# Gated delta rule: key-key and key-query products made once per token tile and kept in SBUF for the other scan direction

## The chip, the cores and the metric

One core of a Trainium2 chip runs the whole program. The metric is the device time of one execution in microseconds; the time of a kernel is the median of its runs.

## What is computed

The reference is a four-layer transformer for one latent sequence of 256 tokens and one context of 256 tokens, all in float32. Layer 1 is a gated delta network with 8 heads of dimension 128, and the change lies in it alone. It is scanned in both directions. For one head, one direction and one chunk, cut to what matters:

```python
decay = where(tri, exp(gc[:, None] - gc[None, :]), 0)     # gc: running sum of the gates, per direction
lmat  = where(strict, (k * beta) @ k.T * decay, 0)
tmat  = inverse(eye + lmat)
a_qk  = q @ k.T * decay
v_new = tmat @ (v * beta) - (tmat @ (k * beta * exp(gc))) @ state
o     = (q * exp(gc)) @ state + a_qk @ v_new
state = state * exp(gc[-1]) + (k * exp(gc[-1] - gc)).T @ v_new
```

`k @ k.T` and `q @ k.T` don't depend on the direction. `beta`, `gc`, the triangle and the state do.

## The kernel before

The kernel is written engine by engine: every engine has its own program, and counted semaphores order them. The 512 tokens are 4 tiles of 128. After the projections of layer 1 comes the scan: the loop over `s` (4 steps) and, inside it, over `hg` (two groups of 4 heads). One pass of the inner loop is called a half-step here; there are 8. A half-step treats both directions d = 0 and d = 1, each on its own tile: `tls = (s, s ^ 1)`, so direction 0 visits tiles 0, 1, 2, 3 and direction 1 visits tiles 1, 0, 3, 2. What direction 0 uses in an even step is thus used by direction 1 in the odd step after it, and the other way round.

PSUM has 8 banks of 128x512. Direction d uses bank 3d, 3d+1 and 3d+2, and bank 6+d. The four heads of a group lie side by side in a bank, 128 columns each. A half-step runs in this order:

- TensorE makes the decay rows (L1607, bank 3d; from the second half-step on each direction waits for its state update `st_upd` first), the key-key products (L1611, bank 3d+1), and behind both directions the key-query products (L1615, bank 3d+2).
- VectorE subtracts and clamps them (L2385, `bD`), ScalarE takes the exponentials (L945 to `bD`, L946 to `bE`), VectorE multiplies decay, -beta and key-key product to `bNL` (L2393, one instruction for each head, the product read from PSUM), then the masked decay with the key-query product to `bAT` (L2400, one 128x512 instruction for each direction).
- GpSimd has two instructions for each direction: it masks the decay (L699, `bAT` from `bD`, as soon as L945 is done) and multiplies `bE` with the queries (L706). All of them read SBUF.
- TensorE inverts by levels: L1636 (needs `bNL`) into bank 3d, which ScalarE copies (L952) to `bA`; key times state (L1624) into bank 6; L1647 and L1651, which need `bAT`'s bank read and `bA`, into banks 3d+1 and 3d+2; L1624 again for the other direction; VectorE copies (L2405, L2408) and adds values (L2417); L1660, L1665 and L1672; then L1680 solves, L1687 and L1688 give the outputs, L1694 the state product, L2435 or L2437 and L2443 store and update (no state update in step 3).

The order within each engine is that of its program text. The matmuls are float32; each one of the source stands as two records in the trace. `w_hi` and `w_lo`, which hold the split weights of the projections, are idle during the scan: GpSimd begins the next split when the last output of the scan is ready. No DMA is issued for the scan.

Of the kernel before, what the change touches and what calls it, by code (L numbers as in the profile page):

```python
# [19 lines left out]
ALU = mybir.AluOpType  # L20
ACT = mybir.ActivationFunctionType
# [5 lines left out]
P = 128  # L27
# [155 lines left out]
def build(nc, a, out):  # L183
    with ExitStack() as ctx:
        top = [nc.sbuf_base + (-nc.sbuf_base) % 64]

        def sb(name, shape, dt=F32, at=None):
            size = int(np.prod(shape[1:])) * (1 if dt == U8 else 4)
            if at is None:
                at = top[0]  # L190
                top[0] += (size + 63) // 64 * 64
            assert at + size <= nc.sbuf_usable_end, (name, at + size)
            return nc.alloc_sbuf_tensor_at(name, shape, dt, offset=at)

        sem = lambda n: ctx.enter_context(nc.semaphore(n))
        banks = ctx.enter_context(nc.psum_tensor("bank", [P, 8, 512], F32))
        bank = [banks[:, i, :] for i in range(8)]
# [11 lines left out]
        WH0 = top[0]  # L209
# [25 lines left out]
        K4 = 2048  # L235
# [37 lines left out]
        bt = [[sb(f"b{n}{d}", [P, 4, P], at=U0 + (3 + 6 * d + i) * K4) for i, n in enumerate(("D", "E", "AT", "NL", "TT", "A"))]  # L273
              for d in range(2)]
        bT = sb("bT", [P, 4, P], at=U0 + 15 * K4)
        Z0, E0 = AR0, AR0 + 32 * K4
        ZF = 32 * 33
        zg, zb = (sb(n, [P, 2, 32], at=B0 + 256 * i) for i, n in ((0, "zg"), (1, "zb")))
# [119 lines left out]
        qd_ready = sem("decayed_queries_ready")  # L398
        kk_ready = sem("key_products_ready")
        kq_ready = sem("query_products_ready")  # L400
        at_ready = sem("attention_ready")
        nl_ready = sem("lower_ready")
        a_ready = sem("level_a_ready")
# [71 lines left out]
        quad = lambda t: t.rearrange("p (a b) -> p a b", a=4)  # L475
# [302 lines left out]
        def _(eng):  # L778
# [86 lines left out]
            def delta_net():  # L865
# [55 lines left out]
                for s in range(TT):  # L921
                    for hg in range(2):
                        first = (s, hg) == (0, 0)
                        for d in range(2):
                            TTm = bt[d][4]
                            th = 8 * (s if d == 0 else s ^ 1) + 4 * hg
                            if first:
                                eng.wait_ge(zt_ready, act.next(zt_ready))
                            else:
                                eng.wait_ge(ty_ready, act.next(ty_ready))  # L930
                            for g in range(4):
                                R = slice(32 * g, 32 * g + 32)
                                turn = lambda t: t[R, :, th:th + 4].rearrange("p c t -> p t c")
                                ins = eng.activation(TTm[R, :, R], turn(bTT32[d]), ACT.Copy)
                                if g // 2 == d:
                                    ins = eng.activation(bT[R, :, R], turn(bT32[d]), ACT.Copy)
                            ins.then_inc(diag_ready, 1)
                        for d in range(2):
                            Dm, E = bt[d][0:2]
                            if (s, hg) == (TT - 1, 1):  # L940
                                eng.wait_ge(od_ready, 14)
                            elif not first:
                                eng.wait_ge(s_done, act.next(s_done))
                            eng.wait_ge(dm_ready, act.next(dm_ready))
                            eng.activation(Dm[:], Dm[:], ACT.Exp).then_inc(dt_ready, 1)  # L945
                            eng.activation(E[:].rearrange("p a b -> p (a b)"), bank[3 * d][:], ACT.Exp).then_inc(e_ready, 1)  # L946
                        for d in range(2):
                            Am = bt[d][5]
                            eng.wait_ge(a_ready, act.next(a_ready))
                            for q in range(2):  # L950
                                S, T = slice(64 * q + 32 * d, 64 * q + 32 * d + 32), slice(64 * q + 32 - 32 * d, 64 * q + 64 - 32 * d)
                                ins = eng.activation(Am[T, :, S], quad(bank[3 * d][T, :])[:, :, S], ACT.Copy)  # L952
                            ins.then_inc(am_ready, 1)
                        for d in range(2):
                            Am = bt[d][5]
                            S, T = slice(64 * d, 64 * d + 64), slice(64 - 64 * d, 128 - 64 * d)
                            eng.wait_ge(a_ready, act.next(a_ready))
                            eng.activation(Am[T, :, S], quad(bank[3 * d][T, :])[:, :, S], ACT.Copy).then_inc(am_ready, 1)
# [244 lines left out]
        def _(eng):  # L1203
# [339 lines left out]
            def delta_net(l):  # L1543
                inside = late_beside(l)
                for p in range(16):
# [10 lines left out]
                    if p == 1:  # L1556
                        ada_late(l, 13, 14, 15)
                        eng.wait_ge(tz_ready, pe.next(tz_ready))
                        for t in range(TT):
                            mm = eng.transpose(bank[6][:, t * B_TAIL:(t + 1) * B_TAIL], btz[:, t * P:(t + 1) * P], ident[0:B_TAIL, 0:B_TAIL])  # L1560
# [16 lines left out]
                    if p == 6:  # L1577
                        eng.wait_ge(hn_ready, pe.next(hn_ready, 2))
                        eng.wait_ge(sm_b, pe.next(sm_b, 2))
                        for th in range(32):  # L1580
                            tl, h = divmod(th, B_HEADS)
                            for g in range(4):
                                blk = bk[:, h, tl * P + 32 * g:tl * P + 32 * g + 32]
                                mm = eng.matmul(bank[4 + th // 16][32 * g:32 * g + 32, th % 16 * 32:th % 16 * 32 + 32], blk, blk, start=True, stop=True)
# [9 lines left out]
                for s in range(TT):  # L1594
                    for hg in range(2):
# [5 lines left out]
                        C = lambda b: slice(b * P, (b + 1) * P)  # L1601
                        for d in range(2):
                            if not first and (s, hg) != (TT - 1, 1):
                                eng.wait_ge(st_upd, pe.next(st_upd))
                            for b in range(4):
                                c = d * B_HEADS + H(b)
                                mm = eng.matmul(bank[3 * d][:, C(b)], b_g[:, tls[d], c:c + 1].to_broadcast([P, P]), con[:, tri[d]:tri[d] + P],  # L1607
                                                start=True, stop=True)
                            mm.then_inc(gb_ready, 1)
                            for b in range(4):  # L1610
                                mm = eng.matmul(bank[3 * d + 1][:, C(b)], bk[:, H(b), tok[d]], bk[:, H(b), tok[d]], start=True, stop=True)  # L1611
                            mm.then_inc(kk_ready, 1)
                        for d in range(2):
                            for b in range(4):
                                mm = eng.matmul(bank[3 * d + 2][:, C(b)], bk[:, H(b), tok[d]], bq[:, H(b), tok[d]], start=True, stop=True)  # L1615
                            mm.then_inc(kq_ready, 1)
# [23 lines left out]
                        for d in range(2):  # L1640
                            TTm, Am = bt[d][4:6]
                            eng.wait_ge(diag_ready, pe.next(diag_ready))
                            eng.wait_ge(at_ready, pe.next(at_ready))
                            eng.wait_ge(am_ready, pe.next(am_ready))
                            for b in range(4):
                                i, o = 96 * d, 32 + 32 * d
                                eng.matmul(bank[3 * d + 1][o:o + 32, b * P + i:b * P + i + 32], TTm[o:o + 32, b, o:o + 32],  # L1647
                                           Am[o:o + 32, b, i:i + 32], start=True, stop=True)
                                for q in range(2):
                                    i, o = 64 * q + 32 * d, 64 * q + 32 - 32 * d  # L1650
                                    mm = eng.matmul(bank[3 * d + 2][i:i + 32, b * P + o:b * P + o + 32], Am[o:o + 32, b, i:i + 32],  # L1651
                                                    TTm[o:o + 32, b, o:o + 32], start=True, stop=True)
                            mm.then_inc(b_ready, 1)
# [9 lines left out]
                        for d in range(2 if s < TT - 1 else 0):  # L1663
                            for b in range(4):
                                mm = eng.transpose(bank[3 * d + 1][:, C(b)], bk[:, H(b), tok[d]], ident)  # L1665
# [328 lines left out]
        def _(eng):  # L1994
# [324 lines left out]
            def delta_net(l):  # L2319
# [53 lines left out]
                for s in range(TT):  # L2373
                    for hg in range(2):
# [12 lines left out]
                        for d in range(2):  # L2387
                            Dm, NLm = bt[d][0], bt[d][3]
                            eng.wait_ge(dt_ready, dve.next(dt_ready))
                            eng.wait_ge(kk_ready, dve.next(kk_ready))  # L2390
                            for b in range(4):
                                c = col(d, b)
                                ins = eng.scalar_tensor_tensor(NLm[:, b, :], Dm[:, b, :], b_nbeta[:, tls[d], c:c + 1],  # L2393
                                                               bank[3 * d + 1][:, C(b)], ALU.mult, ALU.mult)
                            ins.then_inc(nl_ready, 1)
                        for d in range(2):
                            AT = bt[d][2]
                            eng.wait_ge(pat_ready, dve.next(pat_ready))
                            eng.wait_ge(kq_ready, dve.next(kq_ready))
                            eng.tensor_tensor(AT[:], AT[:], quad(bank[3 * d + 2][:]), ALU.mult).then_inc(at_ready, 1)  # L2400
                        for d in range(2):
                            TTm = bt[d][4]
                            eng.wait_ge(b_ready, dve.next(b_ready))
# [400 lines left out]
```

## Time and profile before

| | us |
|---|---|
| median of 3 runs | 2655.36 (2650.93 to 2656.78) |
| the profiled execution: time, span | 2652.73, 2650.6 |
| the scan, within the span | 917.6 to 1082.7 |
| one half-step in the middle of it | 20.73 |

"PEclk" and the granted clock are TensorE's clock as a share of 2.4 GHz; 0.5 is 1.2 GHz. A row of the timeline can merge instructions that follow each other on one engine; "x4" is their number. Start times count from the start of the span.

### The profile page before, as it was taken

To read this page: it belongs to the slowest core of one execution; us is meant where nothing else is said; L and a number is where in the kernel's file an instruction comes from. 1 tells how busy PE (TensorE), PEld (TensorE's weight loads), DVE (VectorE), ACT (ScalarE), POOL (GpSimd) and SP (SyncE) were. 2 spreads that over 40 slices of the span, in tenths; PEclk is the share of its full clock that TensorE was granted. 3 is DMA by queue.
4 is the path that set the end of the run, shared out by engine and by line. 5 is a ranking of instruction groups with operands and counts; after the bars stand their busy time and mean duration, and the time that the engine had idled before them with its cause. 6 is when DMAs were issued, how large, how long until landed. Compare 5 with 4: busy or idle time off the path is not lost.

```text
span 2650.6 us, 43681 instructions
## 1 busy us (share of the span) xinstructions
PE 2499.9 (94%) x15985; PEld 2047.4 (77%) x15985; DVE 1163.4 (44%) x2120; ACT 751.9 (28%) x1539; POOL 1583.5 (60%) x1567
## 2 busy tenths in 40 slices
PE   6999999999999799999999999878999999989997
PEld 4767788887688698778888757866788887678997
DVE  2384411223469677541222330265422223575555
ACT  2263311111541444231111124152311101363332
POOL 2545577775558222457777555685577775655663
PEclk9999999999999899999999999999999999999999
DMA  7345332244523100242224542202432344503552
GB/s 250 113 161 183 109 104 95 96 158 159 177 65 96 32 2 2 95 145 95 95 95 159 174 162 80 64 1 104 136 95 95 99 157 173 193 31 96 185 176 99
DMA packets 217162, 305.07 MB, mean 115 GB/s; under 512 B 7331, under 2 KB 155550, under 8 KB 217023
## 3 DMA queue, kind: packets, MB, share of 16 engines
q1 hardware_dynamic: 190095, 249.66, 28.6%
q10 hardware_dynamic: 26928, 53.48, 5.6%
q8 instruction: 97, 1.59, 0.3%
q14 instruction: 42, 0.34, 0.0%
HBM read 302.07 MB, written 1.05 MB: 114 GB/s over the span
## 4 chain that ended last, share of the span: by engine, by line
PE 79%; DVE 12%; ACT 3%; POOL 3%; issue 2%; DMA 1%; SPq 1%; DVEq 0%; ACTq 0%; POOLq 0%; PEldq 0%
PE bank L1225 42%; PE bank L1934 13%; PE bank L1276 3%; PE bank L1240 2%; PE bank L1965 2%; PE bank L1713 2%; PE bank L1260 2%; PE bank L1763 2%; PE bank L1757 1%; POOL cqf L725 1%; PE bank L1355 1%; PE bank L1331 1%; DVE ast L2130 1%; DVE ztmp L2203 1%; DVE ztmp L2187 1%
## 5 line engine op out<-in xcount | busy, mean ns | idle before, releaser
L656 POOL TENSOR_TENSOR w_lo<-w_raw,w_hi 128x512 fp32r<-128x512 f32 x652 | 856.3, 1313 | 93.7 <-POOL w_hi L653 72.0
L653 POOL TENSOR_SCALAR w_hi<-w_raw 128x512 fp32r<-128x512 f32 x652 | 427.8, 656 | 617.3 <-PE bank L1225 381.7
L1225 PE MATMUL bank<-u_lo,w_hi 128*128 128x512 f32 (+1 forms) x2048 | 758.5, 370 | 10.0 <-DVE u_lo L2051 6.8
L1225 PE MATMUL bank<-u_hi,w_hi 128*128 128x512 f32 (+1 forms) x2048 | 751.6, 367 | 0.0
L1225 PE MATMUL bank<-u_hi,w_lo 128*128 128x512 f32 (+1 forms) x2048 | 751.4, 367 | 0.0
L1225 PEld LDWEIGHTS bank<-u_lo,w_hi 128*128 128x128 f32 x2048 | 389.1, 190 | 90.6 <-issue 18.9
L1225 PEld LDWEIGHTS bank<-u_hi,w_hi 128*128 128x128 f32 x2048 | 388.9, 190 | 63.1
L1225 PEld LDWEIGHTS bank<-u_hi,w_lo 128*128 128x128 f32 x2048 | 389.2, 190 | 61.0
L1934 PE MATMUL bank<-gs_lo,w_hi 128*128 128x512 f32 (+1 forms) x576 | 209.2, 363 | 1.9 <-POOL w_lo L656 1.8
L1934 PE MATMUL bank<-gs_hi,w_lo 128*128 128x512 f32 (+1 forms) x576 | 208.8, 363 | 0.0
L1934 PE MATMUL bank<-gs_hi,w_hi 128*128 128x512 f32 (+1 forms) x576 | 208.8, 363 | 0.0
L2728 DVE TENSOR_TENSOR gs_lo<-g,gs_hi 128x512 fp32r<-128x512 f32 (+1 forms) x88 | 107.6, 1233 | 230.4 <-ACT gs_hi L1172 230.4
L2703 DVE SCALAR_TENSOR_TENSOR cv<-bank,vec,cv 128x510 f32<-128x510 f32 (+1 forms) x88 | 59.6, 677 | 325.6 <-ACT cv L1146 325.4
L1146 ACT ACTIVATE cv<-bank,vec 128x512 f32<-128x512 f32 (+1 forms) x88 | 58.8, 718 | 500.4 <-PE bank L1225 462.1
L2720 DVE TENSOR_TENSOR g<-cv,bank 128x512 f32 (+3 forms) x88 | 50.8, 616 | 197.1 <-PE bank L1225 195.8
L1172 ACT ACTIVATE gs_hi<-g 128x512 fp32r (+3 forms) x88 | 49.4, 574 | 306.1 <-PE bank L1934 249.0
L736 POOL TENSOR_SCALAR ap<-ap,ast 128x512 f32<-128x512 f32 (+1 forms) x48 | 76.3, 1590 | 80.6 <-DVE ast L2141 80.6
L1934 PEld LDWEIGHTS bank<-gs_lo,w_hi 128*128 128x128 f32 x576 | 108.7, 189 | 20.2 <-issue 3.5
L1934 PEld LDWEIGHTS bank<-gs_hi,w_hi 128*128 128x128 f32 x576 | 108.7, 189 | 17.0
L1934 PEld LDWEIGHTS bank<-gs_hi,w_lo 128*128 128x128 f32 x576 | 108.7, 189 | 16.8
L2056 DVE SCALAR_TENSOR_TENSOR x<-bank,gat,x 128x256 f32<-128x256 f32 x112 | 48.6, 479 | 140.9 <-PE bank L1225 74.7
L2089 DVE TENSOR_TENSOR w_lo<-w_raw,w_hi 128x512 fp32r<-128x512 f32 x76 | 68.5, 911 | 89.4 <-ACT w_hi L811 76.0
(350 smaller groups left out, 3755.4 us busy)
## 6 DMA issues: line engine op xcount, KB each, us to landing
w_raw<-in_ffn_w_up SPq DMA_DIRECT2D x88, 1024.0 KB, 5.1
w_raw<-in_ffn_w_down SPq DMA_DIRECT2D x44, 1024.0 KB, 4.9
ada_area<-in_ada_w ACTq DMA_DIRECT2D x39, 1024.0 KB, 15.4
ada_w<-in_ada_w SPq DMA_DIRECT2D x28, 1024.0 KB, 5.2
w_raw<-in_gdn_w_in SPq DMA_DIRECT2D x16, 1024.0 KB, 5.8
w_raw<-in_attn_w_qkv SPq DMA_DIRECT2D x12, 1024.0 KB, 7.9
ada_w<-in_ada_w ACTq DMA_DIRECT2D x12, 1024.0 KB, 6.7
w_raw<-in_gla_w_in SPq DMA_DIRECT2D x12, 1024.0 KB, 5.4
```

What stands on the lines that cost most here:

```text
L653: eng.tensor_scalar(w_hi[:, q, :], src, 1.0, 0.0, ALU.mult, ALU.add).then_inc(pool.own, pool.step())
L656: eng.tensor_tensor(w_lo[:, q, :], src, w_hi[:, q, :].bitcast(F32), ALU.subtract).then_inc(w_split, 1)
L736: eng.tensor_scalar(pj, pj, ast[:, 4, j % 4, 0:1], None, ALU.mult).then_inc(p_ready, 1)
L1146: eng.activation(cv[:, m, T], bank[(PAIR_GATE if pair else 0) + m][:, T], ACT.Identity, bias=vec[:, bass.ds(f + CONVB(l), 1)], scale=vec[: ...
L1225: mm = eng.matmul(bank[banks[m]][:, T], w[:, q, c:c + P], v[:, k, T], start=(k == 0 and n == 0), stop=(k == KT - 1 and n == 2))
L1240: eng.matmul(bank[banks[m]][:, T], w[:, slot, c + m * P:c + (m + 1) * P], u_hi[:, k, T], start=(k == 0 and n == 0), stop=False)
L1260: mm = eng.matmul(bank[banks[m]][:, T], w[:, k // 2, c:c + P], v[:, k, T], start=(k == 0 and n == 0), stop=(k == KT - 1 and n == 2))
L1276: mm = eng.matmul(bank[banks[t]][:, 0:256], v[:, k, t * P:(t + 1) * P], w[:, q, c:c + 256], start=(k == 0 and n == 0), stop=(k == KT - 1 a ...
L1934: mm = eng.matmul(bank[b][:, T], w[:, q, j * P:(j + 1) * P], v[:, s, T], start=(start and q < 2 and n == 0), stop=(stop and q >= 2 and n = ...
L2089: eng.tensor_tensor(w_lo[:, q, :], w_raw[:, s, q * PIECE:(q + 1) * PIECE], w_hi[:, q, :].bitcast(F32), ALU.subtract).then_inc(w_fourth, 1)
L2703: eng.scalar_tensor_tensor(v3(cv[:, m, :], 1, 256), v3(bank[gate + m][:], 0, 255), w0, v3(cv[:, m, :], 1, 256), ALU.mult, ALU.add).then_in ...
L2728: eng.tensor_tensor(gs_lo[:, slot, T], gf, gs_hi[:, slot, T].bitcast(F32), ALU.subtract).then_inc(gs_ready, 1)
```

## The change

In even steps nothing is taken away: TensorE makes both products for both tiles. ScalarE gets four more instructions in each half-step: it copies the key-key product of each direction to `bkk` behind the exponentials and ahead of L952, and the key-query product to `bkq` behind L952. TensorE waits for the copy of a direction (`kp_ready`) ahead of L1647 of that direction. In odd steps TensorE makes neither product; VectorE's L2393 and L2400 read `bkk` and `bkq` of the other direction from SBUF in place of PSUM. The two new tiles lie where `w_hi` and `w_lo` are.

```diff
+        bkk = sb("bkk", [P, 2, 2, 4, P], at=WH0)
+        bkq = sb("bkq", [P, 2, 2, 4, P], at=WH0 + 4 * K4)
+        kept = lambda s, hg: 4 * (s // 2 * 2 + hg)
...
+                        for d in range(2 if s % 2 == 0 else 0):                       # ScalarE, ahead of L952
+                            eng.wait_ge(nl_ready, 4 * s + 2 * hg + d + 1)
+                            eng.activation(bkk[:, hg, d], quad(bank[3 * d + 1][:]), ACT.Copy).then_inc(kp_ready, 1)
...
+                        for d in range(2 if s % 2 == 0 else 0):                       # ScalarE, behind L952
+                            eng.wait_ge(at_ready, 4 * s + 2 * hg + d + 1)
+                            eng.activation(bkq[:, hg, d], quad(bank[3 * d + 2][:]), ACT.Copy).then_inc(kp_ready, 1)
...
-                            for b in range(4):
+                            for b in range(4 if s % 2 == 0 else 0):                   # TensorE, L1611
                                 mm = eng.matmul(bank[3 * d + 1][:, C(b)], bk[:, H(b), tok[d]], bk[:, H(b), tok[d]], start=True, stop=True)
-                            mm.then_inc(kk_ready, 1)
-                        for d in range(2):
+                            if s % 2 == 0:
+                                mm.then_inc(kk_ready, 1)
+                        for d in range(2 if s % 2 == 0 else 0):                       # TensorE, L1615
...
                             eng.wait_ge(at_ready, pe.next(at_ready))                  # TensorE, ahead of L1647
+                            if s % 2 == 0:
+                                eng.wait_ge(kp_ready, kept(s, hg) + 3 + d)
...
-                            eng.wait_ge(kk_ready, dve.next(kk_ready))                 # VectorE, L2393
+                            if s % 2 == 0:
+                                eng.wait_ge(kk_ready, dve.next(kk_ready))
+                                KK = quad(bank[3 * d + 1][:])
+                            else:
+                                eng.wait_ge(kp_ready, kept(s, hg) + 4)
+                                KK = bkk[:, hg, 1 - d]
...
-                            eng.wait_ge(kq_ready, dve.next(kq_ready))                 # VectorE, L2400
-                            eng.tensor_tensor(AT[:], AT[:], quad(bank[3 * d + 2][:]), ALU.mult).then_inc(at_ready, 1)
+                            if s % 2 == 0:
+                                eng.wait_ge(kq_ready, dve.next(kq_ready))
+                            KQ = quad(bank[3 * d + 2][:]) if s % 2 == 0 else bkq[:, hg, 1 - d]
+                            eng.tensor_tensor(AT[:], AT[:], KQ, ALU.mult).then_inc(at_ready, 1)
```

## Rows read from the trace of the kernel before

**Rows 1.** The page: span and busy time of each engine.

```profile
span 2650.6 us, 43681 instructions
PE 2499.9 (94%) x15985; PEld 2047.4 (77%) x15985; DVE 1163.4 (44%) x2120; ACT 751.9 (28%) x1539; POOL 1583.5 (60%) x1567
```

**Rows 2.** The chain that ended last, its pieces in the second half-step: start, us, what.

```profile
941.21 0.89 PE bank L1611 x8
...
944.08 0.88 DVE bNL L2393 x4
...
946.28 0.62 PE bank L1636 x16
...
948.57 1.09 PE bank L1624 x8
```

**Rows 3.** The timeline of that half-step: start, us, engine, line.

```profile
940.36 1.12 DVE L2443 SCALAR_TENSOR_TENSOR bS<-bS,bsm,bank 128x128 f32<-128x128 f32 x4 [0.20 <-PE bank L1694]
...
941.94 1.06 PE L1607 MATMUL bank<-con,bsm 128*128 128x128 f32 x8
...
943.04 1.13 DVE L2385 TENSOR_SCALAR bD<-bank,bsm 128x128 f32<-128x128 f32 x4 [0.52 <-PE bank L1607]
...
943.38 1.27 POOL L699 TENSOR_TENSOR bAT<-bD,con 128x512 f32<-128x512 f32 x1 [15.48 <-ACT bD L945]
...
943.62 1.87 PEld L1615 LDWEIGHTS bank<-bq,bk 128*128 128x128 f32 x16
...
944.08 2.15 DVE L2393 SCALAR_TENSOR_TENSOR bNL<-bD,bsm,bank 128x128 f32<-128x128 f32 x8
...
944.79 0.58 ACT L946 ACTIVATE bE<-bank 128x512 f32<-128x512 f32 x1
...
946.14 1.28 DVE L2400 TENSOR_TENSOR bAT<-bAT,bank 128x512 f32<-128x512 f32 x2
946.19 2.50 POOL L706 TENSOR_TENSOR bE<-bE,bq 128x512 f32<-128x512 f32 x2
946.28 1.22 ACT L952 ACTIVATE bA<-bank 32x128 f32<-32x128 f32 x4 [0.91 <-PE bank L1636]
...
946.84 1.16 PE L1624 MATMUL bank<-bS,bk 128*128 128x128 f32 x8
```

**Rows 4.** The timeline just behind the scan: VectorE and GpSimd, both on SBUF.

```profile
1084.64 1.27 POOL L656 TENSOR_TENSOR w_lo<-w_raw,w_hi 128x512 fp32r<-128x512 f32 x1
1084.83 1.63 DVE L2534 SCALAR_TENSOR_TENSOR bo<-bo,vec,bg 128x512 f32<-128x512 f32 x1 [2.19 <-ACT sq L1050]
1085.88 1.06 POOL L653 TENSOR_SCALAR w_hi<-w_raw 128x512 fp32r<-128x512 f32 x1
1086.39 1.09 DVE L2534 SCALAR_TENSOR_TENSOR bo<-bo,vec,bg 128x512 f32<-128x512 f32 x1
...
1087.03 1.59 POOL L656 TENSOR_TENSOR w_lo<-w_raw,w_hi 128x512 fp32r<-128x512 f32 x1
1087.40 1.76 DVE L2534 SCALAR_TENSOR_TENSOR bo<-bo,vec,bg 128x512 f32<-128x512 f32 x1
...
1093.12 0.75 DVE L2534 SCALAR_TENSOR_TENSOR bo<-bo,vec,bg 128x512 f32<-128x512 f32 x1
```

**Rows 5.** Single lines, ns min/median/max: small and large operations with two SBUF inputs.

```profile
L2567 DVE SCALAR_TENSOR_TENSOR drow<-crow,drow x8: 289/292/294, 268.8 to 2625.4; 128x128 f32<-128x128 f32 x6, 64x128 f32<-64x128 f32 x2
...
L2552 DVE TENSOR_TENSOR u_lo<-bo,u_hi x8: 681/682/1183, 1095.5 to 1105.7; 128x512 fp32r<-128x512 f32 x8
```

**Rows 6.** Stretches: us, busy time of PE, PEld, DVE, ACT, POOL, granted clock, DMA.

```profile
1071.40:1074.80 3.40, 2.61 (x35) 2.28 (x34) 3.31 (x13) 0.76 (x2) 0.00 (x0) 1.00 0.00 0
1074.80:1078.20 3.40, 3.40 (x17) 3.40 (x18) 0.90 (x2) 0.00 (x0) 0.00 (x0) 0.50 0.00 0
```

**Rows 7.** The timeline of L1680, in the last and in the second half-step.

```profile
953.08 2.02 PE L1680 MATMUL bank<-bD,bTT 128*128 128x128 f32 x16 [0.31 <-DVE bTT L2424]
...
1074.70 3.64 PE L1680 MATMUL bank<-bD,bTT 128*128 128x128 f32 x16 [0.79 <-DVE bTT L2424]
```

More of the change, by code:

```diff
@@ L400, in build @@
         kq_ready = sem("query_products_ready")
+        kp_ready = sem("products_kept_for_other_direction")
         at_ready = sem("attention_ready")
@@ L2393, in delta_net @@
                                 ins = eng.scalar_tensor_tensor(NLm[:, b, :], Dm[:, b, :], b_nbeta[:, tls[d], c:c + 1],
-                                                               bank[3 * d + 1][:, C(b)], ALU.mult, ALU.mult)
+                                                               KK[:, b, :], ALU.mult, ALU.mult)
                             ins.then_inc(nl_ready, 1)
```

## The prediction

> **What bounds the kernel now.** I read the page first, for the share of each engine [rows 1]: TensorE is busy 2499.9 of 2650.6 us, and nothing but the scan's own text is edited. Then the chain of waits inside the scan, since a share of busy time says nothing of what a removed matmul is worth there. The second half-step shows the pattern that all repeat [rows 2]: key-key products of direction 0 (and the decay rows of direction 1 and VectorE's L2385 behind them), the eight instructions of L2393 (`bNL`), then TensorE again at L1636. So the key-query products (L1615) are not on the chain: they end about 945.5 while VectorE is still at L2393 until 946.23 [rows 3]. Of the 3.57 us of products in a half-step (0.89 for one direction of L1611 [rows 2], so 1.78, and about as much for L1615) only 0.89 us stand in front of something that the chain needs. The chain changes engines several times in a half-step, and every delay of L2393 reaches the end: from L1636 on it is TensorE, VectorE, TensorE without slack. Third, the timeline of the same half-step, for what each engine does beside the others. Last, the places where VectorE and GpSimd both work on SBUF [rows 4], because that is what the odd steps will do, and the stretches with a lowered clock [rows 6].
>
> **What odd half-steps (4 of 8) gain.** The decay rows of direction 1, which start at 941.94 [rows 3], no longer stand behind 0.89 us of L1611 and could start at 941.05. But they also wait for the state update, L2443, which ends at 941.48 [rows 3]. So they start at about 941.55, and L2385 for direction 1, which waited for them until 943.04 [rows 3], starts at 942.65: 0.4 us sooner. In the last half-step there is no such wait and it is 0.7. Dropping L1615 gives nothing. If all else stayed, the odd half-steps would give 3 x 0.4 + 0.7 = 1.9 us.
>
> **What L2393 pays for reading SBUF.** The instruction by itself is not dearer: with two SBUF inputs of 128x128 the row is 292 ns [rows 5] where eight of L2393 take 2.15 us [rows 3], that is 0.34 for one row and 0.26 us from start to start; a 128x512 product is 682 ns from two SBUF inputs [rows 5] and 0.64 us each for L2400 [rows 3]. I take no difference; the bounds are -0.05 and +0.05 us an instruction.
>
> But GpSimd works at that very time. L699 runs 943.38 to 944.65 and once more before 946.19, when the two of L706 begin, which end at 948.69 [rows 3]; all four read SBUF. What happens when a VectorE instruction with two SBUF inputs meets GpSimd stands right behind the scan [rows 4]: alone, L2534 takes 0.75 us. Issued at 1084.83 while L656 runs until 1085.91, it takes 1.63 us and ends 0.55 us after L656. L653 then takes 1.06 us and the next L2534, issued at 1086.39, ends at 1087.48, again after it; L656 takes 1.59 us in place of 1.27 and the third L2534 1.76. They take turns, one instruction each, whatever their sizes. Today L2393 has one SBUF tensor and one of PSUM and shows no stretch (2.15 us for eight, beside L699).
>
> The Trainium skill has the rule for this, in "SBUF — State Buffer", section "SBUF: two separate sides": a VectorE instruction with two SBUF inputs and a GpSimd instruction that reads SBUF exclude each other for a whole instruction. The trace agrees (1.63 against 0.75 us). The skill's "VectorE: DVE Perf Modes", section on the TRN2 errata, speaks for the change instead: an SBUF source costs 58 cycles where PSUM costs 120, about 65 ns less an instruction, by my estimate 4 x 10 x 0.065 = 2.6 us for the ten instructions of each odd half-step. The rows show 50 ns at 128 columns and nothing at 512, so I don't count on it.
>
> Now the turns in an odd half-step, on the clock of [rows 3]. L2393's first instruction is ready at about 943.7, L699 holds SBUF from 943.38 to 944.65. By [rows 4] a blocked VectorE instruction gets through about 0.13 us before the GpSimd row ends and holds it for its length (0.53 us for 512 columns, so about 0.14 for 128), and the next GpSimd instruction ends 1.26 us after that: a turn is 1.27 us. GpSimd has four instructions queued (dt_ready of direction 1 is there in time), so the four instructions of direction 0 end at about 944.8, 946.1, 947.35 and 948.6. Then GpSimd is empty and the four of direction 1 run freely, 0.26 us each, until 949.65. They ended at 946.23. The delay is 3.4 us, with the gain above already lost in it. L2400 follows at once (until 950.9) and is not late: TensorE has L1636 and 1.1 us of L1624 to do first. GpSimd's L706 ends 0.4 us later than now and has several us of slack. Four times 3.4 is **+13.7 us**. Bounds: VectorE gets all its instructions through after GpSimd's first, +0.4 us each, +1.6 in all; or no exclusion at all, -1.9.
>
> **What the delay does to the clock.** TensorE has nothing to do from the end of the decay rows (about 942.7 to 943.6) to the first `bNL` at 948.6, five us, then 0.6 us of small matmuls. In the last half-step of today a stretch with 2.61 of 3.40 us busy was followed by one at half the clock [rows 6], and L1680 took 3.64 us in place of 2.02 [rows 7]. Five idle us are less work than that, so I expect 1.2 GHz when work resumes, in every odd half-step. One stretch of 3.4 us at half the clock costs at most 1.7 us, and two 3.4; [rows 7] shows 1.6 for one. TensorE is nearly the whole chain from L1636 to L1660, and the stretch will not begin with the work. I take 2.0 us, **+8 us** for four; bounds 0 and 13.6.
>
> **What even half-steps pay.** ScalarE's new instruction has the shape of L946 from PSUM, 0.58 us [rows 3]. The first copy of `bkk` can start at about 945.3 and is free. The second needs all of L2393, 946.23, and runs until about 946.85; L952, which ran 946.28 to 947.50, now ends at 948.0. The two copies of `bkq` end at 948.5 and 949.0. TensorE waits for them ahead of L1647; it came there at 948.00 (end of L1624) [rows 3]. Direction 0 is late by 0.5 us, direction 1 starts at 949.05 and the second L1624, 948.57 [rows 2], by 0.7 us. Behind it stand L1660, L1665 and L1672, and VectorE's L2405 and L2424 wait for TensorE. So +0.7 us, four times: **+2.8 us**. Cover gone entirely (each copy 0.58 on the path) is +1.2, or 4.8; if later idle gaps took it up it would be 0. The memory taken is free: GpSimd's next split waits for the last output. No DMA and no queue is moved.
>
> **The sum.** 13.7 + 8 + 2.8 = 24.5 us. Against the profiled execution, 2652.7 (span 2650.6 and 2.1 around it), this is 2677; that execution lay 2.6 us under the median of the runs, so against 2655.4 it is 2680. I say 2679. What lies behind the scan starts later by the same amount.
>
> **The rivals.**
> - VectorE overtakes: after GpSimd's first instruction all ten of VectorE run together. 4 x 0.4 + 2.8 = 4.4 us, 2660. For it: L2393's instructions are short and queued closely. Against: L2534 was queued the same way (its next starts 0.07 us ahead of the last one's end) and lost every turn. 0.08.
> - No exclusion for this pair: -1.9 + 2.8 = +0.9 us, 2656. Against it is all of [rows 4]; for it only that no row has this very pair. 0.05.
> - Faster: TensorE's own work sets the pace of a half-step, by some order that the chain doesn't show, and 4 x 3.57 = 14.3 us go; with 2.8 paid, 2644. It decides if L1615 is what L1636 waits for: it ends 945.5, L2393's first four instructions 945.1, so for direction 0 that is nearly so, but direction 1's at 946.23 ends the wait. 0.03.
> - Turns as forecast, and the clock stays up: 16.5 us, 2672. It is the lower end of my main case.
>
> **How the numbers follow.** The turns have 0.84, between 2668 and 2690 by the bounds of the clock term (0 to 13.6) and of the copies. The range reaches down to the rival next to it: 2659 to 2690. A difference of 0.2%, 5.3 us, is about what a measurement of this kernel can tell. Slower by more than that: the main case and a little of the first rival, 0.87; within it 0.10; faster 0.03.
>
> **What would show it.** In the profile after: L2393 in odd steps with a maximum near 1.3 us for three or four instructions of eight, and 0.3 for the rest; L699 and L706 stretched to about 1.4; a half-step of some 24 to 26 us in odd steps and 21.4 in even ones; a granted clock under 1 in the odd ones; TensorE waiting for `bNL` about 5 us. I am wrong if L2393's rows stay at 0.34 us, or if the clock stays at 1.00.

## The result, and the profile after

The changed kernel takes 2689.5 us (median of 4, 2683.9 to 2691.9) where the kernel before takes 2653.1: 1.35% slower, ratio 1.0135 (1.0111 to 1.0160), or 36.4 us. (The 2653.1 is the median of four runs, the three of the table ahead of the prediction and one of 2648.2.) The direction was forecast and the time lies inside the range, 0.5 us from its upper end: 24.5 us more were expected, and 2679. The profiled execution, the slowest of the four, has a span of 2689.7 us, 39.1 more than the profile before.

The page's first lines (answering to [rows 1]) show that TensorE executes 128 records less and is busy for longer:

```profile
span 2689.7 us, 43441 instructions
PE 2512.9 (93%) x15857; PEld 2057.3 (76%) x15857; DVE 1180.6 (44%) x2120; ACT 760.2 (28%) x1555; POOL 1583.4 (59%) x1567
```

Below are the eight half-steps of the changed kernel as stretches. The columns are those of [rows 6]: length, busy time of PE, PEld, DVE, ACT and POOL, granted clock, DMA share and GB/s. The first two are step 0, the third and fourth step 1, and so on.

```profile
918.90:947.60 28.70, 27.60 (x249) 26.20 (x250) 17.09 (x45) 10.86 (x26) 5.00 (x4) 0.70 0.01 1
947.60:972.90 25.30, 24.21 (x250) 22.70 (x249) 16.34 (x48) 10.88 (x26) 5.02 (x4) 0.80 0.00 1
972.90:998.80 25.90, 18.54 (x219) 17.04 (x218) 19.93 (x49) 8.71 (x22) 5.07 (x4) 0.80 0.01 1
998.80:1027.40 28.60, 21.79 (x218) 20.08 (x217) 20.07 (x48) 8.71 (x22) 5.07 (x4) 0.70 0.00 1
1027.40:1049.10 21.70, 20.05 (x250) 18.77 (x249) 16.19 (x49) 10.86 (x26) 5.02 (x4) 1.00 0.01 2
1049.10:1070.80 21.70, 20.05 (x251) 18.77 (x250) 16.18 (x49) 10.88 (x26) 5.01 (x4) 1.00 0.01 2
1070.80:1096.50 25.70, 18.89 (x194) 17.46 (x193) 17.00 (x41) 8.65 (x22) 5.07 (x4) 0.67 0.01 1
1096.50:1119.40 22.90, 15.48 (x194) 14.10 (x193) 16.77 (x38) 3.97 (x10) 5.07 (x4) 0.85 0.00 1
```

The same table of the kernel before has 22.6, five times 20.7 (one reads 20.8), 18.3 and 19.8 us; its first and last row:

```profile
917.60:940.20 22.60, 21.85 (x249) 20.67 (x250) 16.90 (x45) 8.70 (x22) 4.99 (x4) 0.92 0.01 2
1062.10:1081.90 19.80, 18.96 (x226) 17.91 (x224) 12.81 (x38) 4.31 (x11) 5.00 (x4) 0.91 0.01 2
```

The scan grew from 164.3 to 200.5 us, 36.2. What lies ahead of it and behind it holds the other 3 us of the two profiles. Three things are seen in the rows. The odd half-steps grew although TensorE has less to do in them. The two even half-steps that run at clock 1.00 grew by 1 us. And wherever a stretch in this table is longer than 22 us, its clock is under 1; even ones are among these.

The timeline of an odd half-step answers to [rows 3] (L2411 was L2393, L703 was L699, L710 was L706, L1647 was L1636, L2420 was L2400):

```profile
976.15 2.54 POOL L703 TENSOR_TENSOR bAT<-bD,con 128x512 f32<-128x512 f32 x2 [20.06 <-ACT bD L949]
976.54 5.88 DVE L2411 SCALAR_TENSOR_TENSOR bNL<-bD,bsm,bkk 128x128 f32<-128x128 f32 x8
...
978.65 2.57 POOL L710 TENSOR_TENSOR bE<-bE,bq 128x512 f32<-128x512 f32 x2
981.43 0.51 PEld L1647 LDWEIGHTS bank<-bT,bNL 32*32 32x32 f32 x16 [6.16 <-DVE bNL L2411]
...
982.35 1.28 DVE L2420 TENSOR_TENSOR bAT<-bAT,bkq 128x512 f32<-128x512 f32 x2
```

The eight instructions took 2.15 us and take 5.88. TensorE stood idle for 6 us. Taken one at a time, three of the first four and the fifth look like this: the first four are long (the fourth, from 980.03, takes 1.34), and the others have their old length once GpSimd's last instruction is over (981.22). GpSimd itself ran on almost undisturbed.

```profile
976.54 1.02 DVE L2411 SCALAR_TENSOR_TENSOR bNL<-bD,bsm,bkk 128x128 f32<-128x128 f32 x1
977.49 1.35 DVE L2411 SCALAR_TENSOR_TENSOR bNL<-bD,bsm,bkk 128x128 f32<-128x128 f32 x1
978.76 1.34 DVE L2411 SCALAR_TENSOR_TENSOR bNL<-bD,bsm,bkk 128x128 f32<-128x128 f32 x1
...
981.30 0.34 DVE L2411 SCALAR_TENSOR_TENSOR bNL<-bD,bsm,bkk 128x128 f32<-128x128 f32 x1
```

The chain of the same half-step (answering to [rows 2]) gives what follows at half the clock: L1635, which was L1624, took 1.09 us and takes 2.00.

```profile
976.63 5.81 DVE bNL L2411 x8
...
983.12 2.00 PE bank L1635 x8
```

The timeline of an even half-step at clock 1.00 shows the copies: `bkk` ends at 1055.81, L959 (which was L952) runs until 1056.96, `bkq` until 1058.06, and TensorE waits 0.89 us.

```profile
1055.21 0.60 ACT L953 ACTIVATE bkk<-bank 128x512 f32<-128x512 f32 x1 [0.40 <-DVE bNL L2411]
...
1055.84 1.12 ACT L959 ACTIVATE bA<-bank 32x128 f32<-32x128 f32 x4
1056.98 1.08 ACT L963 ACTIVATE bkq<-bank 128x512 f32<-128x512 f32 x2
...
1057.83 0.18 PE L1660 MATMUL bank<-bA,bTT 32*32 32x32 f32 x1 [0.89 <-ACT bkq L963]
```

### The profile page after: what moved, and what is told of

It reads as the page before. It is cut to its first block, busy times and chain, and to the rows that moved or that the text cites. A ratio compares the mean times of both kernels' runs of the same rounds, so it can differ in the third digit from the quotient of the medians.

```text
span 2689.7 us, 43441 instructions
## 1 busy us (share of the span) xinstructions
PE 2512.9 (93%) x15857; PEld 2057.3 (76%) x15857; DVE 1180.6 (44%) x2120; ACT 760.2 (28%) x1555; POOL 1583.4 (59%) x1567
## 4 chain that ended last, share of the span: by engine, by line
PE 78%; DVE 12%; POOL 3%; ACT 3%; issue 2%; DMA 1%; SPq 1%; DVEq 0%; POOLq 0%; ACTq 0%; PEldq 0%
PE bank L1235 41%; PE bank L1947 12%; PE bank L1286 3%; PE bank L1250 2%; PE bank L1978 2%; PE bank L1726 2%; PE bank L1776 2%; PE bank L1270 1%; PE bank L1770 1%; POOL cqf L729 1%; DVE bNL L2411 1%; PE bank L1365 1%; PE bank L1341 1%; DVE ast L2143 1%; DVE ztmp L2216 1%
## 5 line engine op out<-in xcount | busy, mean ns | idle before, releaser
L703 POOL TENSOR_TENSOR bAT<-bD,con 128x512 f32<-128x512 f32 x16 | 20.4, 1275 | 164.2 <-ACT bD L949 164.2
```

## The experiments

The theory that they test: the 36 us are the turns that VectorE and GpSimd take at SBUF (3.4 us in each odd half-step), ScalarE's copies (about 1 us in each even one), and a lowered TensorE clock for the rest. The rivals were that one of these parts is the whole, that the copies alone lower the clock, that leaving out TensorE's work does so by itself, or that there is a fourth cause. Times are medians, beside the kernel before on the same chip (2656.1 us for e1 to e4, 2654.4 for e5 to e8, 2653.6 for e9).

**e1, the copies alone.** Edit against the changed kernel: odd half-steps make and read their products as before.

```diff
-                            for b in range(4 if s % 2 == 0 else 0):
+                            for b in range(4):
                                 mm = eng.matmul(bank[3 * d + 1][:, C(b)], bk[:, H(b), tok[d]], bk[:, H(b), tok[d]], start=True, stop=True)
...
-                                eng.wait_ge(kp_ready, kept(s, hg) + 4)
-                                KK = bkk[:, hg, 1 - d]
```

> ScalarE makes the four copies in even half-steps and TensorE waits for them, but odd half-steps make both products again and read them from PSUM, as before the change. My theory: 0.95 us for each of the 4 even half-steps, as two of them took in the profile of after (21.68 against 20.73 us), so 3.8 us over before, about 2657, if the clock stays up; and the odd half-steps stay at 20.73. Rival (the copies alone lower the clock, which would explain the 28.6 and 25.4 us of the even half-steps of step 0): +10 us or more, with a granted clock under 1 in step 0.

Measured: 2666.6 us, 10.5 over before, ratio 1.0037 (1.0023 to 1.0052). The rival was right. Of the four even half-steps of the profile two run at clock 1.00 and take 21.6 and 21.7 us, two run at 0.80 and take 25.6 and 25.4 (one in step 0, one in step 2):

```profile
921.40:947.00 25.60, 24.35 (x249) 22.84 (x250) 16.94 (x45) 10.91 (x26) 4.97 (x4) 0.80 0.01 2
947.00:968.60 21.60, 19.95 (x250) 18.68 (x249) 16.13 (x48) 10.88 (x26) 5.01 (x4) 1.00 0.01 2
1010.10:1035.50 25.40, 24.31 (x250) 22.81 (x249) 16.35 (x48) 10.86 (x26) 5.01 (x4) 0.80 0.00 1
```

A wait of 0.9 us amid the 32-wide matmuls thus costs 0.95 us for itself, and in a half-step that loses the clock up to 3.8 more (25.4 less 20.7 and 0.95).

**e2, the products alone left out.** Edit against the kernel before; steps 1 and 3 read stale PSUM, so their products are missing from the result, and TensorE works on other numbers behind them.

```diff
-                            for b in range(4):
+                            for b in range(4 if s % 2 == 0 else 0):
                                 mm = eng.matmul(bank[3 * d + 1][:, C(b)], bk[:, H(b), tok[d]], bk[:, H(b), tok[d]], start=True, stop=True)
...
-                            eng.wait_ge(kk_ready, dve.next(kk_ready))
+                            if s % 2 == 0:
+                                eng.wait_ge(kk_ready, dve.next(kk_ready))
```

> The products of odd half-steps are left out and VectorE reads whatever lies in the PSUM banks; no copies, no waits for them, no second SBUF input. This leaves out part of the computation: key-key and key-query products of two of the four steps. My theory: the chain gives back 0.4 us in three odd half-steps and 0.7 in the last, 1.9 us under before, 2651, since TensorE is idle for only some 2.5 us in each. Rival 1 (TensorE's own work is the pace): 14 us under before, 2639. Rival 2 (dropping TensorE's work already lowers the clock): odd half-steps of 22 us and more at a clock near 0.8, 5 to 8 us over before.

Measured: 2664.9 us, 8.9 over before, ratio 1.0036 (1.0022 to 1.0050). Rival 2 was right: doing less is slower. The chain did give most of the 0.4 us that was worked out: L2395, which is L2393, begins at 963.42, 3.62 us into the half-step, where it began at 3.93. But the two half-steps of step 1 run at clocks of 0.72 and 0.85 and take 24.7 and 22.1 us, not 20.4:

```profile
959.80:984.50 24.70, 21.62 (x218) 19.83 (x217) 16.33 (x48) 8.70 (x22) 4.99 (x4) 0.72 0.00 1
984.50:1006.60 22.10, 18.47 (x219) 16.97 (x218) 16.18 (x49) 8.73 (x22) 5.01 (x4) 0.85 0.01 1
```

TensorE's wait for `bNL` there is no longer than 2.2 us:

```profile
PE bank L1637 <- DVE bNL L2395: 2.6, 2, 2.2
```

**e3, the idle time filled.** The changed kernel, with products that nobody reads in odd half-steps.

```diff
+                        for i in range(6 if s % 2 == 1 else 0):
+                            d = i % 2
+                            for b in range(4):
+                                eng.matmul(bank[3 * d + 1][:, C(b)], bk[:, H(b), tok[d]], bk[:, H(b), tok[d]], start=True, stop=True)
                         def key_state(d):
```

> The changed kernel, but in odd half-steps TensorE makes six groups of key-key products that nobody reads, 0.89 us each, behind the decay rows, so that it works during VectorE's wait until about 7.8 us into the half-step. VectorE's instructions are those of the changed kernel. If the clock is what makes the delay of 13.7 us into 36: the clock stays at 1.00, odd half-steps take 20.73 + 3.4 = 24.1 us, even ones 21.7, and the time is 3.4 x 4 + 0.95 x 4 = 17.4 over before, 2671, some 19 us faster than the changed kernel though it does more. Rival (the stretch of the odd half-steps is made by something else than the clock): no faster than the changed kernel, 2689 or more.

Measured: 2681.8 us, 25.7 over before, ratio 1.0104 (1.0088 to 1.0120), 8 us under the changed kernel though it does 96 products more (the two intervals overlap by their ends). The half-steps of step 1 are the prediction's term without the clock: at 1.00 they take 24.19 us from one first weight load of L1617 to the next (965.05, 989.24, 1013.42), 3.46 over the 20.73 of before, as worked out. The two of step 3 ran at 0.93 and 0.92. The total is 8 us over the 17.4 expected, mainly because two even half-steps fell to clocks of 0.74 and 0.80 (27.3 and 25.3 us), as in e1.

```profile
965.20:989.30 24.10, 22.04 (x266) 20.61 (x265) 19.91 (x48) 8.72 (x22) 5.11 (x4) 1.00 0.01 1
989.30:1013.50 24.20, 22.15 (x266) 20.68 (x266) 19.96 (x49) 8.74 (x22) 5.10 (x4) 1.00 0.01 2
```

**e7, the second SBUF input alone.** Edit against the kernel before; keys take the place of the product in steps 1 and 3.

```diff
+                                KK = bank[3 * d + 1][:, C(b)] if s % 2 == 0 else bk[:, hg * 4 + b, tls[d] * P:(tls[d] + 1) * P]
                                 ins = eng.scalar_tensor_tensor(NLm[:, b, :], Dm[:, b, :], b_nbeta[:, tls[d], c:c + 1],
-                                                               bank[3 * d + 1][:, C(b)], ALU.mult, ALU.mult)
+                                                               KK, ALU.mult, ALU.mult)
```

> The kernel before with one edit: in odd half-steps L2393 takes a slice of the keys from SBUF in place of the key-key product from PSUM. The lower matrix of steps 1 and 3 is thus another one; all instructions, products and waits are those of before, and no copies are made. It prices the second SBUF input by itself. My theory: bNL of direction 1 at 9.5 us into each odd half-step, odd half-steps of 24.2 us at clock 1.00, 13.8 us over before, 2670; TensorE idles some 3 us in each, so the clock may fall: up to 2680. Rival (the block needs the copies or the removed products too): 2656.

Measured: 2678.3 us, 23.9 over before, ratio 1.0088 (1.0070 to 1.0105). One operand of 32 instructions does two thirds of the damage, with no copy made and no product left out. The mean of the instruction goes from 340 to 765 ns, and the half-steps of step 1 fall to clocks of 0.76 and 0.87, and in the first of them TensorE waits for direction 1's `bNL` until 969.79, 9.6 us after its first decay row (960.18):

```profile
L2394 DVE SCALAR_TENSOR_TENSOR bNL<-bD,bsm,bk 128x128 f32<-128x128 f32 x32 | 22.3, 765 | 0.0
L2394 DVE SCALAR_TENSOR_TENSOR bNL<-bD,bsm,bank 128x128 f32<-128x128 f32 x32 | 8.6, 340 | 0.0
```

```profile
960.20:989.00 28.80, 25.22 (x250) 23.68 (x249) 19.84 (x48) 8.68 (x22) 5.09 (x4) 0.76 0.00 1
989.00:1015.00 26.00, 21.87 (x251) 20.50 (x250) 19.65 (x49) 8.73 (x22) 5.09 (x4) 0.87 0.01 2
```

**e4, GpSimd kept away from bNL.** The changed kernel, with one wait on GpSimd.

```diff
+                        if s % 2 == 1:
+                            eng.wait_ge(nl_ready, 4 * s + 2 * hg + 2)
                         for d in range(2):
                             Dm, AT = bt[d][0], bt[d][2]
                             eng.wait_ge(dt_ready, pool.next(dt_ready))
```

> The changed kernel, but in odd half-steps GpSimd waits for both bNL before its four instructions, so that it and L2393's counterpart never use SBUF at the same time. If the turns with GpSimd are the cause: the eight VectorE instructions go back to 0.34 us a row, bNL of direction 1 is ready 3.8 us sooner; the masked decay is then late and costs about 1 us at L1660's wait, so an odd half-step takes 20.73 + 1 = 21.7 us and the whole 4 + 3.8 = 8 us over before, 2661, if the clock stays up; up to 8 us more where it falls. Rival (a SBUF-sourced operand is itself slow, or the wait for the copies is): the rows stay above 1 us and the time stays at 2689.

Measured: 2691.2 us, 35.2 over before, ratio 1.0139 (1.0123 to 1.0154). Neither came out whole. The rows of bNL are back at 347 ns, so the turns with GpSimd are what made them long. But the time is no better: the masked decay is late, and the `bAT` product, which also has two SBUF inputs now, meets GpSimd's second pair instead and takes 1743 ns in place of 682:

```profile
L2422 DVE TENSOR_TENSOR bAT<-bAT,bkq 128x512 f32<-128x512 f32 x8 | 13.6, 1743 | 5.8 <-POOL bAT L705 5.8
L2413 DVE SCALAR_TENSOR_TENSOR bNL<-bD,bsm,bkk 128x128 f32<-128x128 f32 x32 | 8.7, 347 | 0.0
```

TensorE waits for `bNL` for 2.7 us in all in the first half-step of step 1, where it waited for 6, but it also idles twice ahead of L1662 (the kernel before's L1647, which needs `bAT`), for 1.6 us in all, and the half-steps of step 1 run at 0.70 and 0.69:

```profile
965.50:993.50 28.00, 23.27 (x219) 21.38 (x219) 18.65 (x49) 8.66 (x22) 5.83 (x4) 0.70 0.01 1
993.50:1021.10 27.60, 22.87 (x218) 21.00 (x217) 18.58 (x48) 8.68 (x22) 5.84 (x4) 0.69 0.00 1
```

**e5, the decay read from PSUM.** The changed kernel; GpSimd stays at its time.

```diff
+                            if s % 2 == 1:
+                                eng.activation(quad(bank[3 * d + 1][:]), Dm[:], ACT.Exp).then_inc(dp_ready, 1)
                             eng.activation(Dm[:], Dm[:], ACT.Exp).then_inc(dt_ready, 1)
...
+                            DD = Dm[:] if s % 2 == 0 else quad(bank[3 * d + 1][:])
...
-                                ins = eng.scalar_tensor_tensor(NLm[:, b, :], Dm[:, b, :], b_nbeta[:, tls[d], c:c + 1],
+                                ins = eng.scalar_tensor_tensor(NLm[:, b, :], DD[:, b, :], b_nbeta[:, tls[d], c:c + 1],
```

> The changed kernel, but in odd half-steps ScalarE writes the decay a second time, into the PSUM bank that is free there (3d+1), and L2393's counterpart reads it from PSUM beside the kept product from SBUF: one SBUF input, as before the change, with GpSimd at its old time. If the turns with GpSimd are what blocks it: all rows back to about 0.34 us, bNL of direction 1 ready at about 6 us into the half-step, not 9.5. What is left is the clock that removing the products alone costs (the run that only drops them: 10 us) and the copies (3.8): some 14 us over before, 2670, 20 under the changed kernel. Rival (any SBUF source for the product blocks, whatever the other input): rows above 1 us and 2689.

Measured: 2674.9 us, 20.5 over before, ratio 1.0076 (1.0059 to 1.0094), 15 us under the changed kernel. The row is 342 ns with `bkk` still in SBUF, while GpSimd's L704 runs from 973.55 beside them (973.32 to 975.55 in the first odd half-step), so it takes two SBUF inputs and not one to be held up by GpSimd:

```profile
L2419 DVE SCALAR_TENSOR_TENSOR bNL<-bank,bsm,bkk 128x128 f32<-128x128 f32 x32 | 8.9, 342 | 0.3 <-ACT bank L951 0.3
```

It is 6 us more than expected. The `bAT` product now comes early enough to meet GpSimd (mean 1557 ns), which I had not counted; how the 6 us divide between that and the clock (0.69 to 0.79 in the odd half-steps) isn't shown.

**e6, the same with TensorE busy.** Against e5:

```diff
+                        for i in range(3 if s % 2 == 1 else 0):
+                            d = i % 2
+                            for b in range(4):
+                                eng.matmul(bank[3 * d + 2][:, C(b)], bk[:, H(b), tok[d]], bk[:, H(b), tok[d]], start=True, stop=True)
```

> As the run before it, and in odd half-steps TensorE makes three groups of products that nobody reads, 2.7 us, behind the decay rows. Turns and idle time are both gone, the kept products are still used. If nothing but turns, clock and copies makes the change slow: odd half-steps at clock 1.00 and 20.5 to 20.8 us, the whole 3.8 us over before, up to 10 where the copies lower the clock as they did alone: 2660 to 2666. Rival (a fourth cause): odd half-steps above 21.5 us at clock 1.00.

Measured: 2668.1 us, 13.7 over before, ratio 1.0051 (1.0034 to 1.0067). Two odd half-steps ran at clock 1.00. The one in step 1 took 21.4 us, more than the 20.8 expected and just under the rival's 21.5; the last of the scan took 18.9, where the same half-step of the kernel before takes 18.5 at that clock (e8 and e9). The other two fell to 0.80 and 0.77 and took 25.1 and 22.3. So there is a fourth cause, a small one: 0.4 to 0.7 us in an odd half-step. The rows point to the `bAT` product, which takes turns with L711 and is long enough to delay VectorE's next copies (L2437 follows it at once, at 976.64):

```profile
973.57 3.04 DVE L2432 TENSOR_TENSOR bAT<-bAT,bkq 128x512 f32<-128x512 f32 x2
...
974.34 3.39 POOL L711 TENSOR_TENSOR bE<-bE,bq 128x512 f32<-128x512 f32 x2
```

**e8, the copies with TensorE's next work drawn ahead.** Against e1:

```diff
                         key_state(0)
+                        if s % 2 == 0:
+                            key_state(1)
...
-                        key_state(1)
+                        if s % 2 == 1:
+                            key_state(1)
```

> The copies-only kernel, but in even half-steps TensorE makes the key-state product of direction 1 ahead of the wait for the copies and not behind L1647, so that it works during the wait. Theory (the copies cost 0.95 us each time as a wait, and the rest of their 10 us by the clock, since TensorE waits amid small matmuls): even half-steps of 21.2 to 21.5 us, no half-step of 25 us, 2 to 3 us over before, 2658. Rival (the copies cost 10 us by something else): 2666 as with the copies alone.

Measured: 2660.3 us, 5.9 over before, ratio 1.0027 (1.0014 to 1.0040), 4.6 less over before than e1, though the intervals of the two overlap. The expectation failed: there is a half-step of 25.9 us, and the one even half-step at clock 1.00 is no shorter (21.6 us) than e1's. The wait was only moved: L1675, which is L1660 of the kernel before, now waits for VectorE (0.6 and 0.3 us). In the profiled execution three even half-steps lost clock where e1 has two, 25.9, 24.0 and 23.1 us at 0.79, 0.86 and 0.93; the first lost as much as in e1, the others less. Whether the work during the wait helps is thus not settled.

**e9, the kernel before with work that nobody reads.**

```diff
+                for i in range(12):
+                    eng.matmul(bank[3][:, i % 4 * P:(i % 4 + 1) * P], bk[:, i % 8, 0:P], bk[:, i % 8, 0:P], start=True, stop=True)
                 norm_rows()
+                for i in range(4):
+                    eng.matmul(bank[3][:, i % 4 * P:(i % 4 + 1) * P], bk[:, i % 8, 0:P], bk[:, i % 8, 0:P], start=True, stop=True)
                 eng.wait_ge(conv_done, pe.next(conv_done, 4))
...
+                        for b in range(4 if s == TT - 1 else 0):
+                            eng.matmul(bank[4][:, C(b)], bk[:, H(b), tok[1]], bk[:, H(b), tok[1]], start=True, stop=True)
                         for d in range(2):
                             Dm, TTm = bt[d][0], bt[d][4]
```

> The kernel before with TensorE work that nobody reads where it idles at the ends of the scan: 16 key-key products ahead of the first half-step (in 2.6 and 0.9 us of idle time) and 4 behind L1672 in each of the last two half-steps (0.8 us idle). If work without use keeps the clock up: the first half-step from 22.5 to about 20.8 us, the last from 19.9 to 18.4, 3 us or 0.1% under before, 2652, hardly more than can be measured, but plain in the profile. Rival (added work is only added): 1 to 2 us over before.

Measured: 2647.5 us against 2653.6, ratio 0.9981 (0.9972 to 0.9990): the fastest kernel here, faster than both. The first and the last half-step run at 1.00, and L1680, 3.64 us in [rows 7], takes 1.95:

```profile
918.70:939.50 20.80, 20.08 (x249) 18.88 (x249) 16.66 (x45) 9.53 (x23) 4.97 (x4) 1.00 0.01 2
1061.50:1080.00 18.50, 18.45 (x234) 17.31 (x232) 12.81 (x38) 4.34 (x11) 5.00 (x4) 1.00 0.00 1
```

```profile
1074.28 1.95 PE L1686 MATMUL bank<-bD,bTT 128*128 128x128 f32 x16
```

That is 6 us less, where 3 were expected; the first and the last half-step account for 1.8 and 1.3 in the profiles, and where the rest comes from isn't shown (the interval reaches from 2.7 to 7.4 us). The last half-step is less plain than it looks: in e8's profile, with nothing added there, it also took 18.5 us at 1.00. The same holds for the first: in e7's profile it took 20.8 us at 1.00. The median speaks for the added work; the single half-steps of one profile don't.

## Why the prediction came out as it did, point by point

**The turns: right in mechanism and in size.** The steps said that the first four instructions of L2393 end at 944.8, 946.1, 947.35 and 948.6, on a half-step that begins at 940.15; that is 4.65, 5.95, 7.2 and 8.45 into it. Measured, from 972.93, where TensorE's first decay row starts as it does at 940.15: 4.6, 5.9, 7.2 and 8.4. The last of the eight was put at 9.5 and came at 9.5. At clock 1.00 e3 gives 3.46 us for a half-step against 3.4 in the text, so the term of 13.7 us stands. e7 shows that it needs neither copies nor missing products. e5 shows that one SBUF input beside a PSUM one goes free. The rivals "VectorE overtakes" and "no exclusion" fall with the rows of 1.35 us. Only the stretch of GpSimd's rows was wrong: "about 1.4 us" was forecast and the pairs of L703 and L710 take 2.54 and 2.57 us, nearly their old length. It did not fit the text's own turn of 1.27 us either, which leaves a GpSimd row of 1.4 no room. TensorE's wait for `bNL`, put at 5 us, was 6.

**The copies: right in mechanism, a quarter too small, and one consequence missed.** 0.7 us was the term, 0.95 the measurement (21.68 against 20.73 at clock 1.00), so 3.8 in place of 2.8. The first `bkq` copy ends at 8.5 us into the half-step and TensorE starts 0.25 us later, the second likewise, where I had let it start within 0.05.

**The clock: the step that was mis-sized.** "I take 2.0 us, +8 us for four; bounds 0 and 13.6." The scan's 36.2 us less 13.8 for the turns (4 x 3.46) and 3.8 for the copies leave 18.6 us, by difference (the 3.46 of step 1 is taken for step 3 too). That is over twice the 8 and beyond the term's own upper bound of 13.6. All of it lies in the six half-steps with a clock under 1; the two at 1.00 grew by the copies' wait alone. Two things were wrong in that step. It set at most two lowered stretches after each wait and counted only odd half-steps. In fact the first two half-steps, both even, took 28.7 and 25.3 us at clocks of 0.70 and 0.80: 5.1 and 3.7 us more than before and the copies' 0.95 explain, together nearly half of the 18.6. e1 shows that the copies bring that on alone; there it accounts for 6.7 of 10.5 us. In the odd half-steps the second one alone lost 4.4 us (28.6 less 20.7 and 3.46), where the text allowed 3.4. How the two causes combine is shown only roughly: e1's 10.5 us and e7's 23.9 make 34.4 of the 36.4, but e2's 8.9 does not come on top of them. The single half-steps differ from one execution to the next.

**That the time fell inside the range owes something to luck.** The upper bounds of the three terms, 13.7, 13.6 and 4.8 us, make 32.1, and the measured 36.4 is more. The range reached to 2690, though with 2655.4 for the kernel before these bounds end at 2687.5, and the kernel before turned out at 2653.1 with its fourth run. Without either of these 2.5 and 2.3 us the time would have been outside. The mechanism of the main term was right, the size of the clock term was not.

**Leaving out the products gives nothing: right, and it is worse than that.** The text counted 1.9 us of gain in the chain, and e2 shows an earlier start of 0.3 us in the first odd half-step, while the kernel as a whole comes out 8.9 us slower. The rival "no exclusion for this pair", put at +0.9 us, lacked the clock just so: without any turn e2 alone is 8.9 us over before, and e1's copies alone 10.5. "TensorE's own work sets the pace" has e2 against it: the products of the odd half-steps are gone, TensorE still waits for `bNL`, and the time rises.

**An operand from SBUF is no cheaper.** Rows of L2411 that meet nobody take 0.34 us, as with the operand in PSUM, and the product to `bAT` 677 and 680 ns. The Trainium skill's "VectorE: DVE Perf Modes", section on TRN2 errata, would have an SBUF source cost less; the trace does not agree here:

```profile
L2420 DVE TENSOR_TENSOR bAT<-bAT,bkq 128x512 f32<-128x512 f32 x8 | 5.1, 677 | 0.0
L2420 DVE TENSOR_TENSOR bAT<-bAT,bank 128x512 f32<-128x512 f32 x8 | 5.1, 680 | 0.0
```

That a VectorE instruction with two SBUF inputs and a GpSimd instruction that reads SBUF exclude each other, as the Trainium skill has it in "SBUF — State Buffer", section "SBUF: two separate sides", is what e7 and e5 show (765 ns a row against 342).

**What stays open.** Why some even half-steps with the copies lose the clock and others of the same kernel don't. They hold the same instructions; no run here controls where in time they fall. What TensorE did just before doesn't tell them apart either. In e1, one half-step falls to 0.50 at the end of the first of these two stretches, and its neighbour stays at 1.00 through the second, with the same busy time:

```profile
1015.20:1020.30 5.10, 4.12 (x95) 3.45 (x95) 3.12 (x10) 3.36 (x9) 3.44 (x3) 0.93 0.01 3
1040.60:1045.70 5.10, 4.12 (x97) 3.46 (x97) 3.12 (x10) 3.37 (x9) 3.44 (x3) 1.00 0.01 3
```

Open is also why adding work helps the whole kernel by 6 us, and whether the other numbers that e2 and e7 compute with bear on the clock.

## What to carry to other kernels

Before moving an operand from PSUM to SBUF, count the SBUF inputs that the VectorE instruction then has, and look at what GpSimd does in that window: with two, each instruction queued behind one of GpSimd's here, and the short ones paid most for their size (1.35 us in place of 0.34). Work taken off an engine that isn't the one waited for gives nothing, and on TensorE it can cost: here leaving about 3.6 us of matmuls out of half-steps of 20.7 made them longer (24.7 and 22.1 in e2), and adding matmuls that nobody reads made the kernel 0.2% faster in e9. Price a new wait of TensorE at clock 1.00 first, and then look at the granted clock of the stretch around it, since that was half of the loss.

## What was not expected of the hardware

- The turns are lopsided. Against VectorE instructions of 128 columns GpSimd lost nothing in the pair of L703 (2.54 us, as in e2, where nothing meets it) and 0.07 us in that of L710 (2.57 against 2.50), while VectorE lost about 1 us an instruction. Against those of 512 columns GpSimd lost too: 3.39 us for a pair in e6.
- The granted clock fell to half in half-steps in which TensorE has no long wait. In e1's half-step from 1010.10, where its longest wait is 0.9 us, the clock reads 0.50 from 1020.30 to 1028.80; ahead of that its matmul rows had been busy for 4.12 of 5.10 us, and the neighbour, with the same instructions and the same busy time, stayed at 1.00.
